# Weight products from two float32r matmuls instead of three bf16 ones

## The reference

```python
def adaln_in(x, g, m, i):
    return rmsnorm(x, g) * (1 + m[:, i, 1][:, None]) + m[:, i, 0][:, None]

def swiglu(h, w1, w3, w2):
    return (jax.nn.silu(h @ w1) * (h @ w3)) @ w2

    x = x + 0.5 * m[:, 0, 2][:, None] * swiglu(adaln_in(x, norm_g[l, 0], m, 0),
                                               ffn_w1[l, 0], ffn_w3[l, 0], ffn_w2[l, 0])
```

## Time and profile before

| | |
|---|---|
| median of 3 runs | 1821.88 us (1821.85 to 1822.31) |
| span of the profiled execution | 1820.0 us |
| PE busy | 1787.8 us, 98% |
| DVE busy | 1403.4 us, 77% |
| ACT busy | 984.3 us, 54% |
| read from memory | 417 MB, 230 GB/s over the span |

### The profile page before, as it was taken

How to read it: one execution, slowest core, us unless ns; L and a number is a source line. 1 busy time by engine, 2 the same in 40 slices (tenths; PEclk the granted TensorE clock), 3 DMA queues, 4 the chain that set the end, 5 groups by cost and what they waited for, 6 DMA issues and landing times.

```text
span 1820.0 us, 38652 instructions
## 1 busy us (share of the span) xinstructions
PE 1787.8 (98%) x16324; PEld 1560.2 (86%) x16324; DVE 1403.4 (77%) x2261; ACT 984.3 (54%) x1643; POOL 10.0 (1%) x21
## 2 busy tenths in 40 slices
PE   5999999999999999999999999999999999999998
PEld 4888888888888887888888888888888888878887
DVE  7889789898899987776677667977667766787664
ACT  4645656544654466464465445575446544576443
POOL 0000000000000000000000000000000000000000
PEclk9999999999999999999999999999999999999999
DMA  9899664998499943476756664357665656436661
GB/s 361 327 368 410 216 260 157 354 345 292 171 388 384 341 153 115 163 262 231 242 176 215 207 205 166 132 205 234 207 207 176 219 199 208 163 114 213 207 208 48
DMA packets 85017, 421.00 MB, mean 231 GB/s; under 512 B 9363, under 2 KB 9795, under 8 KB 58094
## 3 DMA queue, kind: packets, MB, share of 16 engines
q1 hardware_dynamic: 82910, 410.59, 63.6%
q0 software_dynamic: 1936, 7.95, 1.2%
HBM read 417.37 MB, written 1.13 MB: 230 GB/s over the span
## 4 chain that ended last, share of the span: by engine, by line
PE 90%; DVE 6%; ACT 2%; issue 1%; DMA 1%; SPq 0%; DVEq 0%; ACTq 0%
PE pw L591 19%; PE pw L592 18%; PE pw L593 18%; PE acc L591 10%; PE acc L592 10%; PE acc L593 10%; DVE ring_lo L1926 1%; DMA biasT<-wmod 1%; PE acc L903 1%; PE pw L861 1%; ACT ring_hi L1421 1%; PE acc L885 1%; PE acc L752 0%; PE acc L647 0%; PE acc L883 0%
## 5 line engine op out<-in xcount | busy, mean ns | idle before, releaser
L591 PE MATMUL pw<-h_hi,ring_hi 128*128 128x256 bf16 x3048 | 831.8, 273 | 2.6 <-DVE biasT L2194 1.1
L593 PE MATMUL pw<-h_hi,ring_lo 128*128 128x256 bf16 x3048 | 831.4, 273 | 0.0
L592 PE MATMUL pw<-h_lo,ring_hi 128*128 128x256 bf16 x3048 | 831.4, 273 | 0.0
L1926 DVE TENSOR_TENSOR ring_lo<-land,ring_hi 128x1024 bf16<-128x1024 f32 x418 | 493.8, 1219 | 37.0 <-ACT ring_hi L1421 36.7
L1421 ACT ACTIVATE ring_hi<-land 128x1024 bf16<-128x1024 f32 x418 | 417.8, 1043 | 48.5 <-DMA land<-stream 17.7
L592 PE MATMUL acc<-a_lo,ring_hi 128*128 128x256 bf16 x1376 | 376.6, 274 | 0.0
L593 PE MATMUL acc<-a_hi,ring_lo 128*128 128x256 bf16 x1376 | 376.6, 274 | 0.0
L591 PE MATMUL acc<-a_hi,ring_hi 128*128 128x256 bf16 x1376 | 376.5, 274 | 0.0
L591 PEld LDWEIGHTS pw<-h_hi,ring_hi 128*128 128x128 bf16 x3048 | 297.8, 98 | 51.7 <-issue 9.0
L592 PEld LDWEIGHTS pw<-h_lo,ring_hi 128*128 128x128 bf16 x3048 | 297.9, 98 | 35.4 <-issue 0.3
L593 PEld LDWEIGHTS pw<-h_hi,ring_lo 128*128 128x128 bf16 x3048 | 297.9, 98 | 34.8
(11 more groups left out here) (358 smaller groups left out, 1731.4 us busy)
## 6 DMA issues: line engine op xcount, KB each, us to landing
land<-stream SPq DMA_DIRECT2D x207, 1024.0 KB, 5.8
land_d<-stream SPq DMA_DIRECT2D x209, 512.0 KB, 3.8
modw<-wmod SPq DMA_DIRECT2D x130, 512.0 KB, 6.7
biasT<-wmod SPq DMA_DIRECT2D x14, 512.0 KB, 12.2
biasT<-bias_rows POOLq DMA_DIRECT2D x3, 1536.0 KB, 10.6
biasT<-bias_rows POOLq DMA_DIRECT2D x1, 3072.0 KB, 17.1
land<-stream SPq DMA_DIRECT2D x4, 512.0 KB, 4.5
cst_s<-cst SPq DMA_DIRECT2D x1, 1792.0 KB, 10.7
```

What stands on the lines that cost most here:

```text
L591: mm(o, lhs[0], rhs[0], start=start, stop=False, skip_group_check=True)
L592: mm(o, lhs[0], rhs[1], start=False, stop=False, skip_group_check=True)
L593: return mm(o, lhs[1], rhs[0], start=False, stop=stop, skip_group_check=True)
L1926: v.tensor_tensor(ring_lo[:, t % RING, b, :], land[:, t % LAND, b, :] if b < 2 else land_d[:, DOWN_NO[t] % LAND, :], ring_hi[:, t % RING, ...
```

## The change

Weights and activations are kept in float32r, a 4-byte format that TensorE reads rounded, and the product has two matmuls. With 63 and 64 as factors the two parts are made so that the first-order rounding errors cancel: the activation's first part is 63a rounded and its second is 64a less the first; the weight's first part is w/64 rounded and its second is w less 63 times the first. First by first plus second by second is then aw.

```diff
-                mm(o, lhs[0], rhs[0], start=start, stop=False, skip_group_check=True)
-                mm(o, lhs[0], rhs[1], start=False, stop=False, skip_group_check=True)
-                return mm(o, lhs[1], rhs[0], start=False, stop=stop, skip_group_check=True)
+                mm(o, lhs[0], rhs[0], start=start, stop=False, skip_group_check=True)
+                return mm(o, lhs[1], rhs[1], start=False, stop=stop, skip_group_check=True)
```

The second part of a weight is written over the landed block itself (`land_p` and `low_p` are one memory), so landing buffer and ring become one, with three pairs and three down blocks:

```diff
-                    v.tensor_tensor(ring_lo[:, t % RING, b, :], land[:, t % LAND, b, :] if b < 2 else land_d[:, DOWN_NO[t] % LAND, :],
-                                    ring_hi[:, t % RING, b, :], ALU.subtract).then_inc(lo_ready, 1)
+                    hi, fine, rows = hi_block(t, b), low_block(t, b), slice(0, P)
+                    if b == 2 and half(t):
+                        fine, rows = hi, slice(P // 2, P)
+                    v.scalar_tensor_tensor(fine[rows], hi[rows], -ONCE, land_block(t, b)[rows], ALU.mult, ALU.add).then_inc(lo_ready, 1)
```

A pair's slot is loaded again when PE has done the up products of the triple three before it, a down slot when its triple's last product is done:

```diff
-                if t >= LAND:
-                    sp.wait_ge(lo_ready, PAIR_SPLIT[t - LAND])
+                if t >= NPAIR:
+                    old = max(i for i in range(NSTAGE) if FIRST[i] <= t - NPAIR)
+                    if t - NPAIR < UNSHIFTED:
+                        sp.wait_ge(bias0_mm, 1 if t == NPAIR else 2)
+                    elif kinds[old] == "ffn":
+                        sp.wait_ge(gu_ready, ffn_no[old] * NFF + t - NPAIR - FIRST[old] + 1)
+                    else:
+                        sp.wait_ge(triple_used, t - NPAIR + 1)
...
-                if n >= LAND:
-                    sp.wait_ge(lo_ready, SPLIT_NO[DOWN_TRIPLES[n - LAND], 2])
+                if n >= NDOWN:
+                    sp.wait_ge(triple_used, DOWN_TRIPLES[n - NDOWN] + 1)
```

```diff
-                steps[i, j] = [(f + j + 1, 2)] + ([(f + j + 3, 0), (f + j + 3, 1)] if j < NFF - 1 else [])
-                if half(f + j + 3):
-                    steps[i, j].pop()
+                steps[i, j] = [(f + j + 2, b) for b in range(1 if half(f + j + 2) else 2)] + [(f + j, 2)]
```

ACT's copy of a block gets a factor:

```diff
-                    fn(ring_hi[:, t % RING, b, :], land[:, t % LAND, b, :] if b < 2 else land_d[:, DOWN_NO[t] % LAND, :],
-                       ACT.Copy).then_inc(hi_ready, 1)
+                    fn(hi_block(t, b), land_block(t, b), ACT.Copy, scale=1.0 / TWICE).then_inc(hi_ready, 1)
```

The same is done for the activations: each first part gets the factor 63 (in the gains, the shifts and the ACT copies), and each second part is a scalar_tensor_tensor with the factor 64 in place of a tensor_tensor, as for `a_lo`:

```diff
-                    v.tensor_tensor(low_act, act_in[0:r, j % 2, :], a_hi[0:r, j % (LAG + 1), :], ALU.subtract).then_inc(act_ready, 1)
+                    v.scalar_tensor_tensor(low_act, act_in[0:r, j % 2, :], TWICE, a_hi[0:r, j % (LAG + 1), :], ALU.mult, ALU.subtract).then_inc(act_ready, 1)
```

More of the change, by code:

```diff
@@ L37 @@
 TOPK = 64
-RING = 4
-LAND = 2
+NPAIR = 3
+NDOWN = 3
 MODR = 4
@@ L119 @@
 SPLIT_NO = {s: n + 1 for n, s in enumerate(SPLITS)}
-PAIR_SPLIT = {t: SPLIT_NO[t, 0 if half(t) else 1] for t in range(NT) if (t, 0) in SPLIT_NO}
+assert len(SPLIT_NO) == len(SPLITS)
 DOWN_NO = {t: n for n, t in enumerate(sorted(t for t, b in SPLITS if b == 2))}
@@ L140, in load_groups @@
 def load_groups():
[L142 to L147, removed]
+    pair_end, down_end, taken = {}, {}, {}
+    for i, (kind, blocks) in enumerate(STAGES):
+        f = FIRST[i]
+        for n in range(-(-blocks // 3)):
+            pair_end[f + n] = 3 * (f + n) + (2 if kind == "ffn" else 3.2)
+            down_end[f + n] = min(3 * (f + n) + 9.0, 3 * (f + NFF) + 0.02 * n) if kind == "ffn" else 3 * (f + n) + 3.2
     for (back, b), some in MOD_AB.items():
         for g, k in some:
-            ahead[g, k] = SPLIT_NO[FIRST[1] + back, b]
+            taken[g, k] = 3 * FIRST[1] + {2: 4.5, 3: 6.0, 8: 21.0}[back]
+    freed = [(pair_end[t - NPAIR], 0, "pair", t) for t in range(NPAIR, NT)]
+    freed += [(down_end[DOWN_TRIPLES[n - NDOWN]] if n >= NDOWN else 0, 0, "down", t) for t, n in DOWN_NO.items() if n]
+    for i in MOD_AT:
+        for j, some in enumerate(MOD_AT[i]):
+            for g, k in some:
+                taken[g, k] = 3 * (FIRST[i] + j) + 2.6
     for i in MOD_AT:
@@ L153, in load_groups @@
             for g, k in ((g, k) for some in MOD_AB.values() for g, k in some):
-                freed.append((max(SPLIT_NO[STEPS[0, NFF - 1][-1]], ahead[g - (k < MODR), (k - MODR) % KD]), 1, "mod", (g, k)))
+                freed.append((max(3 * FIRST[1] + 0.1, taken[g - (k < 2), (k - 2) % KD] + 0.1), 1, "mod", (g, k)))
         for j, some in enumerate(MOD_AT[i]):
             for g, k in some:
-                ahead[g, k] = SPLIT_NO[STEPS[i, j][0]] - 1
-                early = SPLIT_NO[STEPS[i, max(j - 3, 0)][-1]]
-                freed.append((max(early, ahead[g - (k < MODR), (k - MODR) % KD]), 1, "mod", (g, k)))
+                early = 3 * (FIRST[i] + max(j - 3, 0)) + 2.7
+                freed.append((max(early, taken.get((g - (k < MODR), (k - MODR) % KD), 0) + 0.1), 1, "mod", (g, k)))
     freed.sort(key=lambda load: load[0:2])
[L161 to L169, removed]
+    groups = {(i, n): [] for i, (_, blocks) in enumerate(STAGES) for n in range(-(-blocks // 3))}
+    for at, _, what, which in freed:
+        t = int(at // 3)
+        i = max(i for i in range(len(STAGES)) if FIRST[i] <= t)
+        groups[i, t - FIRST[i]].append((what, which))
     return groups
@@ L214, in sem, with take @@
             return ctx.enter_context(nc.semaphore(name))
[L216 to L221, removed]
+        base = -(-nc.sbuf_base // 32) * 32
+        room = [base]
+        def take(size):
+            at, room[0] = room[0], room[0] + -(-size // 32) * 32
+            return at
@@ L222, in build @@
+        condb = at("condb", condb_at, [P, D])
+        gu = at("gu", gu_at, [P, 2, 2, S])
+        ctx.enter_context(nc.sbuf_tensor("arena", [P, (room[0] - base) // 4], F32))
         macc = sb("macc", [P, 2, KD])
         ones = sb("ones", [P, P])
[L224 to L231, removed]
```

346 lines of the change are left out of this document (187 added, 159 removed).

## The result

The kernel after takes 1783.1 us (median; 1778.3 to 1783.7) against 1822.0 us before, a ratio of 0.978 [0.977, 0.980]. It is faster, by 39 us where 151 were forecast, and lies 8 us outside the range. The profiled execution spans 1781.8 us.

What follows compares the result with a forecast made beforehand. PE, busy 98% of the span, was taken as the bound, with DVE's work the next floor. Savings 84 + 30 + 12 + 25 = 151 us gave 1820.0 - 151 + 1.9 = 1671 us, range 1590 to 1775.

Steps and rivals of the forecast that it cites:

- Late stages, 84 us: Ffn stages 6, 8, 9, 11: steps fall to DVE's own 6.53 us; 84 of 90.9 us waiting for PE saved.
- Stage 5, 30 us: Ffn stage 5: PE and DVE nearly tie; 30 us saved of the 38.7 us wait ahead of the gate.
- Stages 0, 2, 3, 12 us: Ffn stages with two modulations a step: DVE nearly full, so only 5, 5 and 2 us saved.
- The bound it did set there, late landings: Stage 0, DMA near its limit: late weight landings lengthen steps, bounded by 0 and 11 us.
- Mixers, 25 us: Stages ab, cd, hy, sw: 35 us saved less 10 us for narrow value products, net 25 us.
- The 35 us: Mixer stages: half of DVE's 68 us idle time there taken as saved.
- Edits at nothing: Scaled subtraction, copies, half units, scalings and SP's loads with the smaller ring: taken to cost 0 us.
- Rival 2: Ring or narrow products eat the gain outside the late stages: 1753 us, half of it 1712; chance 0.18.
- The pitch of 0.112 us: PE: one float32r matmul of 256 columns takes 0.112 us, set by its 4-byte weight load; a product 0.223 us.
- rival 1: PE: float32r needs two cycles a column, 0.215 us a matmul; about 2370 us, chance 0.12.
- The granted clock fell: Sign of a wrong prediction: a granted clock that falls because of PE's gaps; no size given.

Runs made afterwards that it cites:

- experiment 9: The kernel before with only the change's product: two bf16 matmuls, factors 15 and 16, old ring, landing slots and order kept; 1661.5 us, ratio 0.912.
- experiment 6: The bf16 form of the changed kernel (experiment 2) with four pair and four down slots instead of three; 1695.8 us, ratio 0.930.
- experiment 2: The changed kernel with bf16 parts in place of float32r, its three slots and new order kept; 1738.5 us, ratio 0.954.
- experiment 4: The changed kernel with four slots instead of two for the first eight modulation tiles of ab; 1772.2 us, ratio 0.973.
- experiments 1: The kernel before with one of each product's three bf16 matmuls left out, old ring and order kept; 1659.7 us, ratio 0.912.
- the fills: The changed kernel with idle f32 matmuls ahead of ffn up steps: five a step took 1812.8 us, two took 1787.3 us.
- experiment 5: The changed kernel with the second matmul left out of all products of at most 128 moving columns; 1758.8 us, ratio 0.966.
- 10: Experiment 6 with the four modulation slots of experiment 4 and the factors 15 and 16; 1691.3 us, ratio 0.929.

## Why the prediction was wrong

The direction, the bound and the late stages were right. The 112.8 us between the forecast saving and the profiled one (151 against 38.2) fall out by its own terms as 1 + 5 + 37 + 69, and 0.7 at the end:

- **Late stages, 84 us: right**, with some luck in the size. 82.7 us came. DVE's step is 6.44 us (6.53 forecast) with no wait for PE. But experiment 9 gained 96 us there, more than the 90.9 the term started from, and the new order cost 14 of them where the forecast took 7. Two scales, one step apart, in stage 6, on DVE's timeline:

```profile
1014.41 0.68 DVE L2077 TENSOR_TENSOR gu<-pw,rs 128x512 f32<-128x512 f32 x1
...
1020.85 0.68 DVE L2077 TENSOR_TENSOR gu<-pw,rs 128x512 f32<-128x512 f32 x1
```

- **Stage 5, 30 us: nearly right**, 24.6. Experiment 9 has 34 there.
- **Stages 0, 2, 3, 12 us: wrong in stage 0.** Stages 2 and 3 grew by 6.3 us where 10 were forecast as gain (experiment 9, in the old order, has 5.6 of them), stage 0 grew by 18.3. The prediction put the shift products at nothing without a reason: 144 one-column bf16 matmuls before, 0.025 us apart, and 96 two-column float32r ones now, 0.213 us apart, some 17 us more. The bound it did set there, late landings, was for another mechanism, and 6 us of that came as well (experiment 6).
- **Mixers, 25 us: wrong.** They grew by 43.8 us. Along the runs that is 21 us gained (experiment 9), 8 lost from 9 to 6 (order and modulation slots), 37 from 6 to 2 (slots) and 20 from 2 to after (format). The narrow products' own price, +10 us against three bf16 matmuls, was right as PE's work, since their pitch is the 0.112 us that was taken. The 35 us set against it were too many: the 21 of experiment 9 already contain the 10 us that 176 narrow products save in bf16, and float32r takes back 20. Without any loss by the ring about 1 us would be left of the 25, an estimate that adds the steps up.
- **Edits at nothing: the step that failed.** "SP's loads keep their count ... The SP queue holds one waiting load, with the modulations behind it" was argued from the steady ffn step, and in the late stages it holds: ACT waits for no pair there. Elsewhere it does not. ACT's waits for landed blocks grew from 22.6 to 149.5 us, all in stages 0 to 4, hy and sw (those in stages 2 and 3, 32 us, cost nothing). With bf16 parts a fourth slot takes them from 142 to 12 and brings back 43 us, 37 of them in mixers. In ab there is the queue as well: eight modulation loads with a weight pair behind them, 11 us by experiment 4. Before the change four slots served these tiles, and SP issued four modulation loads between two pairs. The prediction said what it would cost "if that cover is gone", but looked for it only in stage 0's DMA share. In ab the DMA share is 0.51: it was a wait for buffers, not for bandwidth.
- **Rival 2 was the right rival, under-priced.** It had the mixers give nothing and the narrow products show for 30 (1753). It held the buffers' cost to a lost gain; it is a loss, 25 us in ab alone.
- **The pitch of 0.112 us: nearly right at 256 columns, 0.120.** Sixteen matmuls from 970.27 to 972.07 us are 15 intervals of 0.120:

```profile
970.27 0.28 PE L624 MATMUL acc<-a_hi,hi_d 128*128 128x256 f32 x1
...
972.07 0.28 PE L625 MATMUL acc<-a_lo,low_d 128*128 128x256 f32 x1
```

 Two cycles a column (rival 1) is excluded. One record each, and the subtraction at 1.220 us, came as written.
- **The granted clock fell**, which the prediction listed as something that would show it wrong. It is not the cause of the whole: experiments 1 and 9 have 0.947 and 0.942 and reach the forecast, and the fills gain nothing. In stage 0 it has a share, some 10 us of the shift products' 20 (experiment 5). What it costs in ab, where it is at 0.83, no run separates.

By cause, along the runs (profiled spans): format 47 us (after to 2), slots 40 (2 to 6), modulation slots with other factors 6 (6 to 10), order, split distance and separate landing slots 30 (10 to 9). Together they are the 122 us between after and experiment 9. The first two are shown by runs that change one thing, the third by one that changes two; the last is what remains, and its cause is argued. The shares hold along this path of runs; another path may divide them otherwise.

## What to carry to other kernels

The saving was the removed matmul, and it needed neither the format nor the ring that came with it: try the arithmetic alone first, in the old layout. Where a buffer is freed one engine later than before, don't judge its cover in the steady loop but at each change of stage and behind each queue that mixes loads, and read the count of slots there. Where an operand gets wider, price the instructions with few columns first: here their cost was the weight load, which they could not hide.

## What the runs showed of the hardware

In these rows the distance between float32r matmuls never falls below about two array cycles for each of the 128 columns of the operand that is loaded as weight, however few columns move; the bare 4-byte weight load of the kernel before has the same 0.111 us. With 128 moving columns at the upper clock level the distance is (1127.75 - 1124.40) / 30 = 0.112 us, where bf16 has 0.056 us:

```profile
1124.40 0.28 PE L625 MATMUL acc<-low_d,h_lo 128*128 128x128 f32 x1
...
1127.75 0.28 PE L625 MATMUL acc<-low_d,h_lo 128*128 128x128 f32 x1
```

With eight it is the same, (1134.17 - 1130.82) / 30 = 0.112 us:

```profile
1130.82 0.25 PE L625 MATMUL pssq<-low_p,h_lo 128*128 128x8 f32 x1
...
1134.17 0.25 PE L625 MATMUL pssq<-low_p,h_lo 128*128 128x8 f32 x1
```

At the lower level it is 0.213 us for two columns (experiment 5) and 0.215 for 256, (253.22 - 252.79) / 2 in ab, with the matmuls of L625 between these:

```profile
252.79 0.42 PE L624 MATMUL pw<-h_hi,hi_p 128*128 128x256 f32 x1
...
253.22 0.41 PE L624 MATMUL pw<-h_hi,hi_p 128*128 128x256 f32 x1
```

A 256-column bf16 product takes no less there; in the kernel of experiment 2, (53.94 - 53.51) / 2:

```profile
53.51 0.42 PE L625 MATMUL pw<-h_lo,low_p 128*128 128x256 bf16 x1
...
53.94 0.42 PE L625 MATMUL pw<-h_lo,low_p 128*128 128x256 bf16 x1
```

So at the lower level float32r costs no more than bf16 where 256 columns move, and more where few do.

The Trainium skill (TensorE: Matmul & The Clock Gate, Wait — 56ns, not 53.3ns?) has 128 columns at 106.7 ns cold and 55.6 ns warm, with a floor near 25 ns between starts however few the columns. The bf16 rows here agree (0.025 us for two columns); the float32r rows lie above both figures: 0.112 us for 128 columns at the upper level and 0.213 us for two at the lower. The measurement decides.
